# Output gains and gate multiplied into the projection's weights by GpSimd, two copies a step on ScalarE, and more of the expert choice inside the attention stage

## What is computed

```python
mod = (c_act @ w_ada[l] + b_ada[l])[:, None, :]
shift1, scale1, gate1, shift2, scale2, gate2 = jnp.split(mod, 6, axis=-1)
...
o_a = dsa_attention(...)          # 8 heads of 64, the 128 best keys of each query
o_b = forgetting_attention(...)   # 8 heads of 64
mixed = jnp.concatenate([rms_norm_2(o_a, g_out_a[l]), rms_norm_2(o_b, g_out_b[l])], axis=-1)
x = x + gate1 * (mixed @ w_out[l])
h2 = rms_norm_2(x, g_ffn[l]) * (1.0 + scale2) + shift2
x = x + gate2 * peer_ffn(h2, w_peer_q[l], peer_keys1[l], peer_keys2[l], peer_u[l], peer_v[l])
```

## Time and profile before

| | |
|---|---|
| median of three runs | 4333.61 us (4332.75 to 4339.43) |
| the profiled execution, its own time | 4334.02 us |
| its span in the profile | 4332.2 us |
| TensorE busy | 3776.8 us (87%) |
| VectorE busy | 1706.8 us (39%) |
| ScalarE busy | 626.6 us (14%) |
| GpSimd busy | 1095.9 us (25%) |
| attention stage | about 2821 to 2966 us |
| expert stage | 2966 us to the end |

### The profile page before, as it was taken

One profiled execution on the slowest core, in us unless ns is written; L12 is line 12 of the kernel. 1 busy time (PEld: TensorE's weight loads), 2 busy tenths in 40 slices (PEclk: granted clock), 3 DMA queues, 4 the chain that ended last, 5 costly groups with the idle time before them and its releaser, 6 DMA issues. The chain is left out here.

```text
span 4332.2 us, 45502 instructions
## 1 busy us (share of the span) xinstructions
PE 3776.8 (87%) x17099; PEld 2506.9 (58%) x17106; DVE 1706.8 (39%) x3683; ACT 626.6 (14%) x1566; POOL 1095.9 (25%) x1162
## 2 busy tenths in 40 slices
PE   7989999999989999999999996998866777666666
PEld 3465777744747888888999993465422222222222
DVE  2051231013730000000000004748887776877655
ACT  1121000013520000000000003143211111111011
POOL 0010000001400000000000000003667777777775
PEclk9989999999989999999999998989888888888888
DMA  3143675230019888898777764036899999999998
GB/s 114 48 166 120 229 257 189 98 136 0 20 68 275 306 294 303 306 311 298 254 258 250 257 215 140 25 103 240 337 392 386 418 416 414 419 416 416 419 415 355
DMA packets 549127, 1092.57 MB, mean 252 GB/s; under 512 B 37577, under 2 KB 336982, under 8 KB 548870
## 3 DMA queue, kind: packets, MB, share of 16 engines
q1 hardware_dynamic: 395802, 539.66, 36.8%
q0 software_dynamic: 150768, 546.25, 31.3%
q10 hardware_dynamic: 2428, 5.03, 0.3%
HBM read 1069.55 MB, written 21.30 MB: 252 GB/s over the span
## 5 line engine op out<-in xcount | busy, mean ns | idle before, releaser
L3224 PE MATMUL banks<-peer_ring,consts 128*128 128x512 f32 x1512 | 846.9, 721 | 372.8 <-DMA peer_ring<-in_peer_v_dram,peer_expert 372.8
L3224 PEld LDWEIGHTS banks<-peer_ring,consts 128*128 128x128 f32 x1512 | 339.2, 232 | 875.1 <-DMA peer_ring<-in_peer_v_dram,peer_expert 465.2
L3425 DVE SCALAR_TENSOR_TENSOR peer_ring<-peer_ring,banks 128x1024 f32<-128x1024 f32 x512 | 594.1, 1217 | 252.4 <-DMA peer_ring<-in_peer_u_dram,peer_expert 251.5
L3128 POOL DMA_INDIRECT peer_ring<-in_peer_u_dram,peer_expert x512 | 482.4, 942 | 546.3 <-POOLq L2745 347.1
L3128 POOL DMA_INDIRECT peer_ring<-in_peer_v_dram,peer_expert x512 | 490.6, 958 | 170.1 <-issue 142.5
L2014 DVE TENSOR_TENSOR experts_hid<-experts_gs,banks 128x128 f32<-128x128 f32 (+1 forms) x224 | 66.7, 298 | 1175.9 <-ACT experts_gs L1984 1175.9
L1891 PEld LDWEIGHTS banks<-rows_xt,experts_wg 128*128 128x128 f32 x3584 | 446.9, 192 | 45.2 <-issue 45.1
L1891 PE MATMUL banks<-rows_xt,experts_wg 128*128 128x128 f32 (+1 forms) x3584 | 462.3, 282 | 11.3 <-DMA experts_wu<-in_moe_w_up_dram 9.3
L1891 PE MATMUL banks<-rows_xt,experts_wu 128*128 128x128 f32 (+1 forms) x3584 | 461.3, 282 | 0.0
L1891 PEld LDWEIGHTS banks<-rows_xt,experts_wu 128*128 128x128 f32 x3584 | 441.2, 192 | 0.0
L405 PE MATMUL banks<-xT,proj_w 128*128 128x512 f32 (+1 forms) x720 | 319.6, 601 | 8.2 <-PEq L3576 4.8
(11 more groups left out here) (506 smaller groups left out, 3754.7 us busy)
## 6 DMA issues: line engine op xcount, KB each, us to landing
experts_wg<-in_moe_w_gate_dram SPq DMA_DIRECT2D x112, 1024.0 KB, 5.2
experts_wu<-in_moe_w_up_dram SPq DMA_DIRECT2D x112, 1024.0 KB, 7.7
experts_wd<-in_moe_w_down_dram SPq DMA_DIRECT2D x112, 1024.0 KB, 8.1
ada_w<-in_w_ada_dram SPq DMA_DIRECT2D x12, 2048.0 KB, 7.9
ffn_wg<-in_ffn_w_gate_dram SPq DMA_DIRECT2D x22, 1024.0 KB, 7.8
ffn_wu<-in_ffn_w_up_dram SPq DMA_DIRECT2D x22, 1024.0 KB, 10.4
ffn_wd<-in_ffn_w_down_dram SPq DMA_DIRECT2D x22, 1024.0 KB, 11.8
y_rows<-blank SPq DMA_DIRECT2D x1, 12288.0 KB, 41.8
```

The costliest lines, as they stand in the source:

```text
L3128: pool.indirect_dma_start(out=ring[:, slot_of(kind, n, b), :], out_offset=None, in_=tables[kind == "value"], in_offset=bass.IndirectOffset ...
L3224: last = nc.tensor.matmul(ps[bank + hf][:, :], diag[:, n % 2 * B + b, :], ring[:, slot_of("value", n, b), hf * 512:(hf + 1) * 512], start= ...
L3425: nc.vector.scalar_tensor_tensor(row, row, 1.0, rows_at, ALU.mult, ALU.mult, accum_out=acts[:, t % 2, at:at + 1]).then_inc(dotted[q].sem, 1)
```

## The change

Four edits. (1) The gains and the gate row are no longer applied to the data. A new GpSimd program in the attention block, `fold`, multiplies each loaded w_out half in place, eight 512-column slices, each by the gate row and then, after a wait on that result, by a column of gains; three loads, so 48 multiplies. The gains are loaded as a column for each slice. TensorE waits for the folded weights in place of the loaded ones, in both stages. (2) VectorE's head scalings become `tensor_scalar` with the root alone, and the join is one sum of `h` and the bank. (3) From pair 24 on, ScalarE copies both heads' turned probabilities. (4) From step 28 to 32, two pieces of the choice are run a step.

```diff
+    def fold(self, pool):
+        nc, gate, n = self.S.nc, self.M.rows, 0
+        pool.wait_ge(self.got_gains.sem, self.got_gains.at(32))
+        for c, loads in ((0, 1), (1, 1), (1, 2)):
+            pool.wait_ge(self.out_loaded[c].sem, self.out_loaded[c].at(16 * loads))
+            for k in range(KD):
+                w = self.rooms[c][:, k, :]
+                nc.gpsimd.tensor_tensor(w, w, gate[:, 0, c * 512:(c + 1) * 512], ALU.mult).then_inc(self.gated.sem, 1)
+                n += 1
+                pool.wait_ge(self.gated.sem, self.gated.at(n))
+                nc.gpsimd.tensor_tensor(w, w, self.out_gain[:, k:k + 1].broadcast_to([P, 512]), ALU.mult).then_inc(self.folded.sem, 1)
...
-            sp.dma_start(self.out_gain[:, hf * 512:(hf + 1) * 512], src.partition_broadcast(P)).then_inc(self.got_gains.sem, 16)
+                sp.dma_start(self.out_gain[:, hf * 4:(hf + 1) * 4], src.rearrange("(k p) -> p k", p=P)).then_inc(self.got_gains.sem, 16)
...
-            pe.wait_ge(self.out_loaded[c].sem, self.out_loaded[c].at(16))
+            pe.wait_ge(self.folded.sem, self.folded.at(KD * (c + 1)))
...
-            nc.vector.scalar_tensor_tensor(mix[:, 0, sl], mix[:, 0, sl], rr[:, hf:hf + 1], self.out_gain[:, sl], ALU.mult,
-                                           ALU.mult).then_inc(self.ready.sem, 1)
+            nc.vector.tensor_scalar(mix[:, 0, sl], mix[:, 0, sl], rr[:, hf:hf + 1], None, ALU.mult).then_inc(self.ready.sem, 1)
...
-            nc.vector.tensor_tensor(mix[:, 0, sl], bank[:, :], M.rows[:, 0, sl], ALU.mult).then_inc(self.scaled.sem, 1)
-            dve.wait_ge(self.scaled.sem, self.scaled.at(c + 1))
-            nc.vector.tensor_tensor(S.h[:, 0, sl], S.h[:, 0, sl], mix[:, 0, sl], ALU.add).then_inc(self.joined.sem, 1)
+            nc.vector.tensor_tensor(S.h[:, 0, sl], S.h[:, 0, sl], bank[:, :], ALU.add).then_inc(self.joined.sem, 1)
...
         for i in range(22, 33):
             yield i
             next(K.first)
+            if i >= 28:
+                next(K.first)
...
+            @block.gpsimd
+            def _(pool):
+                first_tile.fold(pool)
...
-                        nc.scalar.activation(pT[:, j % 2, 1, 0:K], ps[5][:, 0:K], ACT.Copy).then_inc(copied_act.sem, 1)
+                        for hd in ((0, 1) if j >= ON_ACT else (1,)):
+                            nc.scalar.activation(pT[:, j % 2, hd, 0:K], ps[4 + hd][:, 0:K], ACT.Copy).then_inc(copied_act.sem, 1)
...
-                        pe.wait_ge(out_loaded[1].sem, out_loaded[1].at(32))
+                        pe.wait_ge(folded.sem, folded.at(3 * KD))
```

More of the change, by code:

```diff
@@ L2549, in begin @@
         self.squares, self.inverse, self.roots, self.ready = (S.sig("v_" + x) for x in ("squares", "inverse", "roots", "ready"))
-        self.turned, self.turned_out, self.mixed, self.scaled, self.joined = (
-            S.sig("v_" + x) for x in ("turned", "turned_out", "mixed", "scaled", "joined"))
+        self.turned, self.turned_out, self.mixed, self.gated, self.folded, self.joined = (
+            S.sig("v_" + x) for x in ("turned", "turned_out", "mixed", "gated", "folded", "joined"))
         self.h_squares, self.h_inverse, self.h_roots, self.h_normed = (S.sig("v_h_" + x) for x in ("squares", "inverse", "roots", "normed"))
@@ L2559, in load @@
         sp.dma_start(keys[:, 64:128], a["peer_keys2_2"][0]).then_inc(self.got_keys.sem, 16)
-        for hf, src in enumerate((a["g_out_a_2"][0], a["g_out_b_2"][0])):
-            sp.dma_start(self.out_gain[:, hf * 512:(hf + 1) * 512], src.partition_broadcast(P)).then_inc(self.got_gains.sem, 16)
+        with self.S.nc.allow_non_contiguous_dma(reason="1024 gains, one a row of the output weights"):
+            for hf, src in enumerate((a["g_out_a_2"][0], a["g_out_b_2"][0])):
+                sp.dma_start(self.out_gain[:, hf * 4:(hf + 1) * 4], src.rearrange("(k p) -> p k", p=P)).then_inc(self.got_gains.sem, 16)
         def out_weights(c):
@@ L2734, in attention_stage, with copied_to @@
         rinv = S.sb("row_inv", [P, N, 2], F32, st)
+        ON_ACT = 24
+        def copied_to(n, hd):
+            if n <= ON_ACT:
+                return (copied_act.sem, copied_act.at(n)) if hd else (copied_dve.sem, copied_dve.at(n))
+            return copied_act.sem, copied_act.at(ON_ACT + 2 * (n - ON_ACT) - (1 - hd))
         def keys_of(i):
@@ L2779, in _ @@
                             if j >= 1:
-                                copied = copied_act if hd else copied_dve
-                                pe.wait_ge(copied.sem, copied.at(j))
+                                pe.wait_ge(*copied_to(j, hd))
                             for kt in range(pairs[j][1] + 1):
@@ L2793, in _ @@
                         for hd in range(2):
-                            copied = copied_act if hd else copied_dve
-                            pe.wait_ge(copied.sem, copied.at(j + 1))
+                            pe.wait_ge(*copied_to(j + 1, hd))
                             h = 2 * hp + hd
@@ L2861, in _ @@
                         K = keys_of(j)
-                        dve.wait_ge(turned.sem, turned.at(2 * j + 1))
-                        if j >= 2:
-                            dve.wait_ge(summed.sem, summed.at(j - 1))
-                        nc.vector.tensor_copy(pT[:, j % 2, 0, 0:K], ps[4][:, 0:K]).then_inc(copied_dve.sem, 1)
+                        if j < ON_ACT:
+                            dve.wait_ge(turned.sem, turned.at(2 * j + 1))
+                            if j >= 2:
+                                dve.wait_ge(summed.sem, summed.at(j - 1))
+                            nc.vector.tensor_copy(pT[:, j % 2, 0, 0:K], ps[4][:, 0:K]).then_inc(copied_dve.sem, 1)
                         if j % 4 == 3:
@@ L2980, in peer_stage @@
     squares, inverse, roots, ready = (S.sig("v_" + x) for x in ("squares", "inverse", "roots", "ready"))
-    turned, turned_out, mixed, scaled, joined = (S.sig("v_" + x) for x in ("turned", "turned_out", "mixed", "scaled", "joined"))
+    turned, turned_out, mixed, folded, joined = (S.sig("v_" + x) for x in ("turned", "turned_out", "mixed", "folded", "joined"))
     h_squares, h_inverse, h_roots, h_normed = (S.sig("v_h_" + x) for x in ("squares", "inverse", "roots", "normed"))
@@ L3394, in join @@
                     dve.wait_ge(mixed.sem, mixed.at(u + 1))
-                    nc.vector.tensor_tensor(acc[:, sl], ps[out_bank[u]][:, :], M.rows[:, 0, sl], ALU.mult).then_inc(scaled.sem, 1)
-                    dve.wait_ge(scaled.sem, scaled.at(u + 1))
-                    nc.vector.tensor_tensor(h[:, t, sl], h[:, t, sl], acc[:, sl], ALU.add).then_inc(joined.sem, 1)
+                    nc.vector.tensor_tensor(h[:, t, sl], h[:, t, sl], ps[out_bank[u]][:, :], ALU.add).then_inc(joined.sem, 1)
                 def invert_h(t):
@@ L3408, in scale_heads @@
                         sl = slice(hf * 512, (hf + 1) * 512)
-                        nc.vector.scalar_tensor_tensor(mix[:, t, sl], mix[:, t, sl], rr[:, t, hf:hf + 1], out_gain[:, sl], ALU.mult,
-                                                       ALU.mult).then_inc(ready.sem, 1)
+                        nc.vector.tensor_scalar(mix[:, t, sl], mix[:, t, sl], rr[:, t, hf:hf + 1], None,
+                                                ALU.mult).then_inc(ready.sem, 1)
                 for t in range(1, TT):
```

1 line of the change is left out of this document (removed).

## The result

The changed kernel took 4349.4 us (median of 7 runs, 4345.6 to 4358.4) against 4334.0 us of the kernel before, beside it on the same chip (7 runs, 4332.8 to 4339.4). The ratio is 1.0033, with a 95% interval of 1.0024 to 1.0043: slower by a third of a per cent. The profiled execution has a span of 4347.5 us, 15.3 more than before. The forecast was 4354, within 4329 to 4376.

What follows compares the result with a forecast made beforehand. Transfers bound the expert stage once its gathers run; TensorE's chain sets their start, so only work ahead counts. 10 + 2 + 5.8 + 4.5 - 2.2 = +20.1 us on 4333.6 gives 4354, range 4329 to 4376.

Steps and rivals of the forecast that it cites:

- Part 1: Projection in the attention stage: TensorE stalls 10 us for GpSimd's fold at the second half, plus 2 us for the clock.
- Part 2: Attention stage's end: VectorE's last take 5.8 us later through early pieces, plus 4.5 us of contention with GpSimd.
- Part 3: Start of the expert stage: little of VectorE's saving lies on TensorE's chain, gain 2.2 us, bounds 0 and 6.
- 16.8 us of work less on VectorE: Expert stage's start: VectorE loses 10.6 us of pieces, 4.3 of multiplies, and 6 x 0.32 at the head scaling.
- (a): Rival: GpSimd slow throughout, 1.68 us an operation, larger stall and tail, +43 us, 4376; chance 0.16.
- (b): Rival: nearly nothing; weights land early, stall 4, no clock loss, tail +3, +3 to +8 us, 4339; chance 0.18.
- (c): Rival: faster, VectorE bounds the expert stage's start, so the whole 16.8 us comes back, -10 us, 4324; chance 0.10.

Runs made afterwards that it cites:

- Edit 4 alone: Kernel before with only the early choice added, two pieces a step at steps 28 to 32: 4341.1 us, ratio 1.0016.
- the two kernels with additions: Changed kernel with TensorE's first expert-stage query product made three times, 4359.6 us; changed kernel with eight unneeded VectorE products before its dots of group 3, 4353.6 us.
- pieces moved without the fold: Kernel before with the eight copies on ScalarE, two choice pieces at steps 26 and 27, none at 31 and 32: 4335.8 us, ratio 0.9999.
- all but edit 4: Changed kernel without the early choice, so one piece a step: 4336.1 us, ratio 1.0007.
- edits 1 and 2: Kernel before with the fold and the shorter VectorE operations alone, copies on VectorE, one piece a step: 4341.1 us, ratio 1.0013.
- pieces moved: Changed kernel with eleven choice pieces as before, but two at steps 26 and 27 and none at 31 and 32: 4339.3 us, ratio 1.0007.

## Why the prediction was right, and where it was not

The time, the sign and the place of most of the loss came out; the tail was right, and that the total came within 5 us is luck beyond it. +12 at the projection, +10.3 in the tail, -2.2 in the expert stage were forecast; +2.2, +9.7 and +0.6 were measured. The attention stage was to be 22.3 us longer and is 12.0.

**Part 1, the stall: mechanism right, size wrong by 8.6 us.** TensorE waited for GpSimd's fold at the second half, 1.41 us (1.3 to 2.3 in the other kernels with the fold, none in one), and not 10, nor did the clock fall: the second group took 7.13 us, before 7.09. Three terms make up the difference. The two halves took 38.0 us (2841.51 to 2879.49) and not 41.6, because the second multiply of a pair took 1.04 us and not 1.27: -3.6. The fold began 16.7 us after the stage's start and not 20.5: -3.8. The two gains' loads answer to the earlier trace rows; loads by line, kernel after:

```profile
L2562 SPq DMA_DIRECT2D consts<-in_g_out_a_dram x1: 435/435/435, 2829.7 to 2829.7; - x1
L2562 SPq DMA_DIRECT2D consts<-in_g_out_b_dram x1: 508/508/508, 2830.2 to 2830.2; - x1
...
DMA to landing us min/median/max: 4.2/4.5/4.8
```

1024 pieces of four bytes cost hardly more to issue (0.44 and 0.51 us) than the gains did before, where the router's 1024 pieces had taken 3.13; the nearest row was not near. That is 2.2 of the 3.8 us. The rest is the landing: the first half of w_out landed 10.8 us after its issue at 2830.71, where 12.3 was given. And TensorE itself came 1.1 us later to its first half. One operation of VectorE ahead of it, in order of time, kernel after:

```profile
2854.65 0.98 DVE L2702 TENSOR_SCALAR first_ss<-first_ss 128x2 f32<-128x2 f32 x1 [1.97 <-ACT xT L2653]
```

Its two columns took 0.17 us before. The two head scalings behind it, which were to be shorter, took 1.67 us together, 1.42 before. The sharing with GpSimd was foreseen and called hidden in the stall; with a stall of 1.4 us it is seen. 10.0 - 3.6 - 3.8 - 1.1 = 1.5. The Trainium skill, "GPSIMD Engine Reference", section 3.1, had led to a stall of some 5 us by its price, an estimated 1.12 us a multiply. The rows had 1.27 and 1.04, a mean of 1.15: for the pair the skill's price was nearer than 1.27 twice, for the multiply by the gate row it was not.

**Part 2, the tail: right within a microsecond as a sum.** Forecast 5.8 + 4.5 = 10.3; measured 11.95 - 2.2 = 9.7. Inside it: contention 4.5 forecast, 3.9 measured (the kernel without the third fold, and five rows that add to it). The Trainium skill's sentence on two-input instructions beside GpSimd ("SBUF — State Buffer", section "Who interferes with whom") agrees: L2515 took 1.68 us beside the fold and 0.69 without it. But L2484, one of the operations that the forecast counted on, was not stretched, and two casts with one input (L2483, L2512) were, of which that sentence says nothing: the sum of 4.5 was near, its members were partly others. The pieces' own price was 5.8, counted on VectorE with the copies off it, and it is 5.7: from the masks of step 29 to the end of the last take it is 18.4 us before (2947.81 to 2966.21) and 24.1 in the kernel without the third fold. Edit 4 alone cost 8.5, since four copies of 0.61 us were still on VectorE in that stretch (26.8 us). The forecast had nothing on TensorE's wait for the take that the pieces hold back (4.44 us) and on the clock that falls behind it. In the kernel after this cost nothing, since VectorE ends later still; in the two kernels with additions, whose last take waited for the slow sums, it was 2.4 us. The copies were costed at nothing on ScalarE; that held, and they gained 1.3 us alone and some 4 beside the fold (5.4 less the 1.4 at the projection). So the tail's loss is the early pieces first, GpSimd's company second.

**Part 3, the expert stage: +0.6 in the two profiles, where -2.2 was forecast.** The gap before u = 6 did fall, from 1.97 us to 0.66. In this execution it was given back on the way, at the lower clock: a turn before the queries took 1.97 us against 1.09, the queries 23.30 against 22.72. The other kernels tell it better, since four have the expert stage of before and five that of after. The last two halves of the projection (u = 6) start 43.1 to 44.2 us after the join with the old code (before, edit 4 alone, copies alone, pieces moved without the fold) and 41.2 to 42.3 with the new one (after, all but edit 4, edits 1 and 2, no third fold, pieces moved): a mean of 1.8 us sooner, the forecast's term. The first value sums come 115.6 to 117.2 us after the join with the old code and 114.2 to 116.3 with the new one, a mean of 0.8 sooner. So the gain is there, but half of it is lost in the turns behind it, and it is smaller than the spread of one execution. The larger point stands: 16.8 us of work less on VectorE (an estimate, worked out in the prediction) moved the first value sums by a microsecond. The length of GpSimd's stop tells nothing: it is 7.92 to 7.94 us in all eleven kernels, even where TensorE came 8.6 us later, because the dots that free the gathers ahead of it were late as well (in that kernel GpSimd had stood 12.71 us for them). The early pieces alone did not make the stage start any faster (117.1 us against 115.6).

**The rivals.** (a), GpSimd slow throughout, fell at once: its multiplies never left 1.04 to 1.47 us. (b), nearly nothing, had the first half right (weights early, hardly a stall, no clock loss there) and the tail wrong. (c), faster because VectorE bounds the start, fell by the two additions: 10.4 us on TensorE cost 10.4 from the first query on, 10.0 on VectorE 2 to 3. The forecast's total was good by luck in part: a stall too large by 10 us, clock included, stood beside a gain that hardly came, and 3.3 us of the 15.3 are no more than the spread ahead of the stage.

No kernel here beats the kernel before by more than the measurement tells: the copies alone have 0.9994 (0.9984 to 1.0003).

## What to carry to other kernels

Where a stage ends in a join of all engines, work moved onto the engine that ends it last is paid there (8.5 of 10.6 us for the five pieces alone), and work saved beyond the join is worth only what lies on the next chain: here VectorE paid for 5 pieces in a stage that it bounds, and saved 16.8 us in one that TensorE bounds. When a side job is put early "in the gaps", look not at the busy shares but add up the engine's own rows from the last place where it waits to the join: here 24.1 us against 18.4, which the forecast had to a few tenths of a microsecond. Then look for the first instruction of another engine that waits for what now stands behind it (here TensorE for a take), for its loss comes on top as soon as that engine ends last. A side engine that reads the same memory, GpSimd here, should be given its work where the other engine has idle time behind it; the third fold cost nothing in the tail with one piece a step and the copies on ScalarE, and 3.9 us with two pieces.

## What the runs showed of the hardware

- A GpSimd multiply of 128x512 f32 in place took 1.27 us with a second full operand and 1.04 us with one column spread over 512; with a wait on its own result between two operations, pairs followed each other in 2.34 us where VectorE did not interfere, and the wait cost next to nothing.
- Beside it even tiny VectorE operations stretch: a cast of 64 columns from 0.19 to 1.23 us, an operation on 2 columns from 0.17 to 0.98, a 512-column multiply from 0.69 to 1.68. What is added (0.5 to 1.0 us in the kernel after, up to 1.1 in the others) is no more than one GpSimd operation of 1.27 us lasts; the small ones suffer most in share. Others in the same stretch kept their time (L2484, 0.68 us, while GpSimd's multiply took 1.47 instead of 1.04).
- Two loads of 512 four-byte pieces were issued in 0.44 and 0.51 us and landed after 4.2 to 4.8 us.
- After TensorE had stood idle 4.0 to 4.5 us in a stage that keeps it busy otherwise, the next 16 value sums took 3.6 us, not 1.9 (four kernels, after among them; its granted clock was then 0.50). The length of the idle time alone does not decide: after 3.41 us of it (the kernel without the third fold) they still took 2.00, with the clock at 0.55 only later, and after 1.84 us (edits 1 and 2 alone) they took 3.64, at a granted clock of 0.54 falling to 0.50. In the same stage code the last 32 sums took 3.68 us in the kernel after and 6.93 in the two kernels with additions.
